# A hybrid decoder step with 64 routed experts: a sixth weight buffer in the place of the residual, and evictions ahead of the wait for weights

## The reference

```python
def sublayer_pair(x, c, mixer, w_ada, b_ada, g1, g2, g3, g4, moe_w):
    ...
    x = x + gt_m * rms_norm(m, g2)
    f = moe(rms_norm(x, g3) * (1 + sc_f) + sh_f, *moe_w)
    x = x + gt_f * rms_norm(f, g4)
    return x, new_state

def moe(h, w_router, router_bias, we_gate, we_up, we_down, ws_gate, ws_up, ws_down):
    ...
    _, top_idx = lax.top_k(scores + router_bias.astype(jnp.float32), TOP_K)
    top_w = top_s / jnp.sum(top_s, axis=-1, keepdims=True) * ROUTED_SCALE
    y = routed_experts(xf, top_idx, top_w, we_gate, we_up, we_down) + swiglu(xf, ws_gate, ws_up, ws_down)
```

## Time and profile before

| | |
|---|---|
| median of 3 runs | 1822.84 us (1821.18 to 1824.63) |
| profiled execution | 1818.75 us, its span 1817.0 us |
| TensorE (PE) busy | 1579.9 us, 87% |
| VectorE (DVE), ScalarE (ACT), GpSimd (POOL) busy | 29%, 23%, 17% |
| weights of 64 experts | 3 loads of 1024 KB each, 9.6, 11.8 and 8.7 us from issue to landing (median) |
| half copy of gate and up (L1982) | 52 times, 2294 ns |

### The profile page before, as it was taken

The page is one execution under the profiler, slowest core; times in us unless marked ns, Lnnn a source line. Parts: engine busy times, 40 slices in busy tenths (PEclk is TensorE's granted clock), DMA queues, the critical chain, the costliest instruction groups (busy, mean ns, idle before and its releaser), DMA issues.

```text
span 1817.0 us, 22427 instructions
## 1 busy us (share of the span) xinstructions
PE 1579.9 (87%) x7179; PEld 890.1 (49%) x7180; DVE 530.0 (29%) x951; ACT 410.7 (23%) x802; POOL 304.1 (17%) x322
## 2 busy tenths in 40 slices
PE   4389999999898999996888799899999998688955
PEld 1057888777755777773454233333333333222311
DVE  2120000146651111111664232323233232112227
ACT  2110000246430000002332132222232322112311
POOL 0030150002000000000111132222232221011244
PEclk8589999958989999998899899999999999888977
DMA  8882498164379743497152698988689988878487
GB/s 278 314 296 35 103 330 295 49 194 163 123 252 291 232 157 106 158 334 236 42 219 72 252 386 335 367 345 333 255 321 403 388 322 329 342 297 349 188 310 249
DMA packets 139202, 456.55 MB, mean 251 GB/s; under 512 B 13241, under 2 KB 78265, under 8 KB 109996
## 3 DMA queue, kind: packets, MB, share of 16 engines
q1 hardware_dynamic: 116541, 326.64, 49.1%
q0 software_dynamic: 22608, 129.18, 20.4%
HBM read 422.44 MB, written 106.92 MB: 291 GB/s over the span
## 4 chain that ended last, share of the span: by engine, by line
PE 76%; DMA 9%; issue 4%; SPq 3%; DVE 3%; POOL 2%; ACT 1%; another core or an unknown queue 1%; DVEq 0%; ACTq 0%; POOLq 0%
PE bank L2067 69%; DMA arena<-in_we_down 4%; PE bank L2596 3%; POOL arena L1148 2%; PE bank L2617 1%; SPq L780 1%; PE bank L2273 1%; DMA arena<-in_cache_b 1%; PE bank L2232 1%; DMA arena<-in_w_ada 1%; DMA arena<-in_w_in 1%; DMA mods<-arena 1%; DMA pscale<-in_pool_scale 1%; DMA yrows<-arena 1%
## 5 line engine op out<-in xcount | busy, mean ns | idle before, releaser
L2067 PE MATMUL bank<-arena 128*64 (+10 forms) x6096 | 1427.6, 517 | 144.8 <-DMA arena<-in_w_ada 30.2
L2067 PEld LDWEIGHTS bank<-arena 128*64 128x64 f32 (+3 forms) x6096 | 756.5, 174 | 714.4 <-issue 503.9
L1982 DVE COPY arena<-arena 128x4096 f32 x52 | 119.3, 2294 | 493.8 <-PE bank L2067 365.5
L1166 ACT ACTIVATE arena<-bank 128x512 f32<-128x512 f32 (+6 forms) x152 | 75.2, 505 | 355.2 <-PE bank L2067 219.7
L1106 POOL COPY icol<-arena 128x1 uint32 (+1 forms) x54 | 86.8, 1608 | 398.2 <-PE bank L2596 397.5
L1498 DVE COPY arena<-bank 128x512 f32<-128x512 f32 (+6 forms) x70 | 41.9, 606 | 210.5 <-PE bank L2067 186.1
L1420 ACT ACTIVATE arena<-arena 128x2048 f32 x52 | 99.3, 1910 | 13.3 <-issue 13.3
L1430 ACT ACTIVATE arena<-bank 128x256 f32<-128x256 f32 x52 | 20.0, 384 | 322.9 <-PE bank L2067 232.1
L1067 POOL DMA_DIRECT2D out<-in_cache_b x24 | 12.0, 507 | 447.2 <-PE bank L2067 446.9
L2596 PEld LDWEIGHTS bank<-ident,arena 128*128 128x128 f32 x416 | 51.0, 194 | 44.7 <-issue 44.7
L1305 ACT ACTIVATE arena<-bank 128x288 f32<-128x288 f32 x48 | 19.7, 411 | 233.6 <-PE bank L2067 233.6
(11 more groups left out here) (234 smaller groups left out, 709.2 us busy)
## 6 DMA issues: line engine op xcount, KB each, us to landing
arena<-in_we_gate SPq DMA_DIRECT2D x64, 1024.0 KB, 9.6
arena<-in_we_up SPq DMA_DIRECT2D x64, 1024.0 KB, 11.8
arena<-in_we_down SPq DMA_DIRECT2D x64, 1024.0 KB, 8.7
out<-in_cache_b POOLq DMA_DIRECT2D x8, 4080.0 KB, 15.0
yrows<-arena POOLq DMA_DIRECT2D x52, 512.0 KB, 9.2
arena<-in_w_ada SPq DMA_DIRECT2D x12, 2048.0 KB, 17.4
arena<-in_cache_b SPq DMA_DIRECT2D x18, 1024.0 KB, 7.9
arena<-in_w_in SPq DMA_DIRECT2D x7, 2048.0 KB, 15.4
```

Source lines behind the costliest of these rows:

```text
L1166: act.activation(out, pick(bank), ACT.Copy).then_inc(emptied["A"], 1)
L1982: dve.tensor_copy(whalf[:, 0:4096], arena[:, bass.ds(base, 4096)]).then_inc(gu_copied, 1)
L2067: return pe.matmul(out, lhsT, rhs, start=first, stop=last)
```

## The change

Three edits come together. The ring has six buffers; the sixth lies where `x1` was, so each tile of `x1` is also written to DRAM (`x1rows`) in the residual stage and loaded back when the sixth buffer's last expert is done. `ysh` moves into the fifth buffer and is loaded when that buffer's last expert is done, with the gates. In the loop, ScalarE loads the register values ahead of silu and waits for the weights behind its eviction; VectorE loads the address first and makes the half copy behind its eviction and the silu product. The tables for six buffers no longer fit one bank, so they take two (`bexp` 0 and 1).

```diff
-RING = 5
+RING = 6
...
-    fill(("bexp",), "D")
+    fill(("bexp", 0), "D")
+    fill(("bexp", 1), "D")
...
+        x1rows = nc.dram_tensor("x1rows", [TOK, D], F32, kind="Internal").ap()
...
-        ysh = mixed
+        ysh = at(A_W0 + 6144, TILES, D)
...
-        RING_AT = (A_W0, A_W1, A_M, 0, A_W0 + 6144)
+        RING_AT = (A_W0, A_W1, A_M, 0, A_W0 + 6144, A_ST + 6144)
...
-        g2mod = at(A_M + 2048, 2, D)
+        g2mod = [at(A_W0 + 6144 + TILES * D, D), at(A_ST + 6144, D)]
...
                 sp.dma_start(h2rows[toks(t), :], hbuf2[0:n, t % 2, :]).then_inc(h2_out, 16)
+                sp.dma_start(x1rows[toks(t), :], x1[0:n, t, :]).then_inc(x1_out, 16)
...
             expert_weights(4, slice(4, 5), None)
+            sp.wait_ge(x1_out, 16 * TILES)
+            sp.wait_ge(ysh_out[1], 32)
+            expert_weights(5, slice(5, 6), None)
...
+            for n in (4, 5):
+                e = NE - NE % RING - RING + n
+                done = sp.value_load(blocki[0:1, DONE + e:DONE + e + 1], min_val=2, max_val=NBLK + 2)
+                sp.wait_ge(d_done, done)
+                sp.sem_inc(load_ticks, 1)
+                if n == 4:
+                    for t in range(TILES):
+                        sp.dma_start(ysh[0:parts(t), t, :], yshared[toks(t), :]).then_inc(ysh_in, 16)
+                    sp.dma_start(g2mod[0], mods[0:1, 5, :].broadcast_to([P, D])).then_inc(g2_in, 16)
+                else:
+                    for t in range(TILES):
+                        sp.dma_start(x1[0:parts(t), t, :], x1rows[toks(t), :]).then_inc(x1_in, 16)
+                    sp.dma_start(g2mod[1][0:NS, :], sample_rows(5)).then_inc(g2_in, 16)
...
             sp.sem_inc(weights_idle, 1)
-            for t in range(TILES):
-                sp.dma_start(ysh[0:parts(t), t, :], yshared[toks(t), :]).then_inc(ysh_in, 16)
-            sp.dma_start(g2mod[:, 0, :], mods[0:1, 5, :].broadcast_to([P, D])).then_inc(g2_in, 16)
-            sp.dma_start(g2mod[0:NS, 1, :], sample_rows(5)).then_inc(g2_in, 16)
...
-            def weights_wait(i, off):
-
-                due = [act.value_load(entry(i, off + DUE + NBLK * n), min_val=1, max_val=NE // RING + 2)
-                       for n in range(RING)]
+            def weights_due(i, off):
+
+                return [act.value_load(entry(i, off + DUE + NBLK * n), min_val=1, max_val=NE // RING + 2)
+                        for n in range(RING)]
+
+            def weights_wait(due):
+
                 for n in range(RING):
                     act.wait_ge(wexp_in[n], 48 * due[n])
                 act.sem_inc(weights_in, 1)
...
             with act.Fori(0, last) as i:
                 for off in (1, 2):
                     turned(i, off - 1)
-                    weights_wait(i, off + 1)
+                    due = weights_due(i, off + 1)
                     silu(i, off)
                     rows(i, off + 1)
+                    weights_wait(due)
                     result(i, off - 1)
...
-            empty(("bexp",), blocki[0:1, 0:DONE], lambda b: b[0:1, 0:DONE])
-            wait_emptied(dve, ("bexp",))
+            for n in range(2):
+                empty(("bexp", n), blocki[0:1, DONE // 2 * n:DONE // 2 * (n + 1)], lambda b: b[0:1, 0:DONE // 2])
+            wait_emptied(dve, ("bexp", 1))
...
-            def copy_gate_up(i, off):
+            def lower_base(i, off):
+
+                return dve.value_load(entry(i, off + NBLK), min_val=0, max_val=RING_AT[2])
+
+            def copy_gate_up(base, i, off):
 
                 dve.wait_ge(weights_in, 2 * i + off + 1)
-                base = dve.value_load(entry(i, off + NBLK), min_val=0, max_val=RING_AT[2])
                 dve.tensor_copy(whalf[:, 0:4096], arena[:, bass.ds(base, 4096)]).then_inc(gu_copied, 1)
...
             with dve.Fori(0, last) as i:
                 for off in (1, 2):
-                    dve.wait_ge(gu_done, 2 * i + off + 2)
-                    copy_gate_up(i, off + 1)
+                    base = lower_base(i, off + 1)
                     rows_half(i, off + 1)
                     product(i, off)
+                    copy_gate_up(base, i, off + 1)
                     result(i, off - 1)
...
                         dve.wait_ge(g2_in, 16 * 2)
+                        dve.wait_ge(x1_in, 16 * TILES)
```

More of the change, by code:

```diff
@@ L510, in build @@
         tabi = arena[:, A_R + 2952:A_R + 2953].bitcast(I32)
[L511 to L514, removed]
+        sixes = at(A_R + 2780, 16)
+        ringrow = at(A_R + 2796, RING)
+        sidehot = at(A_R + 2804, 2, RING)
+        donei = arena[0:1, A_R + 2820:A_R + 2820 + NE].bitcast(I32)
         weigh = at(A_R + 2964, TOPK * NE)
@@ L585, in build @@
                              "at_ready", "d_done", "y_act", "y_dve"))
+        x1_out, x1_in = sem("x1_out"), sem("x1_in")
         weights_in, g2_in, g_used = sem("weights_in"), sem("g2_in"), sem("g_used")
@@ L665, in build @@
         blocki = arena[:, A_R + 2144:A_R + 2144 + DONE + NE].bitcast(I32)
-        assert DONE <= 512 and 2144 + DONE + NE <= 2720
+        assert DONE <= 1024 and 2144 + DONE + NE <= 2780
         def wait_keys_used(eng, f):
@@ L1445, in _ @@
             act.wait_ge(ysh_out[1], 32)
-            weights_wait(0, 0)
+            weights_wait(weights_due(0, 0))
             rows(0, 0)
-            weights_wait(0, 1)
+            due = weights_due(0, 1)
             silu(0, 0)
             rows(0, 1)
+            weights_wait(due)
             with act.Fori(0, last) as i:
@@ L1894, in _ @@
                 dve.memset(ringrow[:, n:n + 1], float(RING_AT[n]))
-            link(dve.tensor_scalar(fives, iota[:, 0:16], float(RING), None, ALU.mult))
+            link(dve.tensor_scalar(sixes, iota[:, 0:16], float(RING), None, ALU.mult))
             link(dve.tensor_scalar(iotab, iota[:, 0:NBLK], float(P), None, ALU.mult))
@@ L1940, in _ @@
             for n in range(2):
-                link(dve.tensor_scalar(prod[:, NE * n:NE * n + 13], fives[:, 0:13], order[:, n:n + 1], None,
+                link(dve.tensor_scalar(prod[:, NE * n:NE * n + 13], sixes[:, 0:13], order[:, n:n + 1], None,
                                        ALU.is_le, ALU.add, accum_out=quo[:, n:n + 1]))
@@ L1953, in _ @@
             link(dve.tensor_scalar(blocki[0:1, DONE:DONE + NE], donei, 7, None, ALU.logical_shift_right))
-            link(dve.tensor_scalar(bexpf[:, 7:8], ends[:, NE - 1:NE], 255.0, None, ALU.add))
+            link(dve.tensor_scalar(bexpf[:, 8:9], ends[:, NE - 1:NE], 255.0, None, ALU.add))
             one_hots(3)
-            link(dve.tensor_copy(tabi, bexpf[:, 7:8]))
+            link(dve.tensor_copy(tabi, bexpf[:, 8:9]))
             link(dve.tensor_scalar(pairs[:, 0:1], tabi, 8, None, ALU.logical_shift_right))
@@ L2004, in _ @@
             dve.sem_inc(y_dve, 1)
-            copy_gate_up(0, 0)
+            copy_gate_up(lower_base(0, 0), 0, 0)
             rows_half(0, 0)
-            dve.wait_ge(gu_done, 2)
-            copy_gate_up(0, 1)
+            base = lower_base(0, 1)
             rows_half(0, 1)
             product(0, 0)
+            copy_gate_up(base, 0, 1)
             with dve.Fori(0, last) as i:
                 for off in (1, 2):
-                    dve.wait_ge(gu_done, 2 * i + off + 2)
-                    copy_gate_up(i, off + 1)
+                    base = lower_base(i, off + 1)
                     rows_half(i, off + 1)
                     product(i, off)
+                    copy_gate_up(base, i, off + 1)
                     result(i, off - 1)
@@ L2056, in _ @@
                         dve.wait_ge(g2_in, 16 * 2)
-                    link(dve.scalar_tensor_tensor(y, y, st, g2mod[0:r, s, :], ALU.mult, ALU.mult))
+                        dve.wait_ge(x1_in, 16 * TILES)
+                    link(dve.scalar_tensor_tensor(y, y, st, g2mod[s][0:r, :], ALU.mult, ALU.mult))
                     dve.tensor_tensor(x1[0:r, u, :], x1[0:r, u, :], y, ALU.add).then_inc(f_out, 1)
@@ L2571, in _ @@
             block_rows(4)
-            bank = bank_for(pe, ("bexp",))
             pe.wait_ge(bexp_ready, 1)
             for n in range(2 + RING):
-                ins = mm(bank[0:1, n * NBLK:(n + 1) * NBLK], bexpf[:, n:n + 1], ident[:, 0:NBLK], True, True)
-            close(ins)
+                m = n % 4
+                if m == 0:
+                    bank = bank_for(pe, ("bexp", n // 4))
+                ins = mm(bank[0:1, m * NBLK:(m + 1) * NBLK], bexpf[:, n:n + 1], ident[:, 0:NBLK], True, True)
+                if m == 3:
+                    close(ins)
             shared_down(3)
```

## The result

| | before | after |
|---|---|---|
| median of the runs | 1823.74 us (1821.18 to 1825.07, 4 runs) | 1746.03 us (1743.38 to 1752.75, 4 runs) |
| profiled execution, span | 1818.75 us, 1817.0 us | 1746.22 us, 1744.5 us |
| TensorE busy | 1579.9 us, 87% | 1574.5 us, 90% |

The ratio is 0.9585, 95% interval 0.956 to 0.961.

The account below looks back on a forecast made before the run. TensorE's own pace was taken as the bound, 12.63 us per block, with halts where the weight ring is full. From 1818.75: -56.2 + 6 - 6.3 = -56.5 gives 1762.2; the median stands 4.1 above: 1766, range 1753 to 1792.

Parts of the forecast that it names:

- the cost per block where nothing halts: Expert loop, new order: half copy stays covered by the down product, so 0 per block; a gain was excluded.
- halts (-56.2, residue +6): Expert loop waits for `we_down`: 56.2 us of excess go with the sixth buffer and new order, 6 us remain: -50.
- tail: Loop's end: with the loads gone ahead, the last yrows store lands in 2.9 us, not 9.2: -6.3 us.
- start: Ahead of block 0: one register load, +0.45, against VectorE's, -0.52, and two-table fill: 0; x1 stores hidden.
- My upper bound: Blocks 37 to 48: transfers need 164 us against 151.6 of blocks, so without lead 12.4 us of halts would stay.
- the six halts: Chain of before: `we_down` landings of 12 to 13 us at 1163.69, 1606.02 and four more between them.
- Copy and gather: Rival: VectorE's half copy and GpSimd's gather collide on the shared port, 0.35 us in about 45 blocks: 1782; chance 0.08.
- Rivals: Slot buys little, 1788, 0.12; copy and gather collide, 1782, 0.08; slot buys nothing, 1799, 0.04; half copy on path, 1830, 0.04.
- the three signs of being wrong: Blocks without a halt above 12.8 us; the half copy in each block's chain; halts left at more than three blocks.

Follow-up runs that it names:

- e1: The kernel before, five buffers, with only the changed order on ScalarE and VectorE (half copy last, behind eviction and product): 1789.61 us, ratio 0.9792.
- e3: The kernel before, with TensorE's register load of the next gate/up weights' place moved ahead of the silu-product wait in every second block: 1818.35 us, ratio 0.9966.
- e4: The changed kernel, with VectorE's half copy between the eviction and the silu product instead of behind the product: 1783.1 us, ratio 0.976.
- e7: The kernel before, with TensorE's register load ahead of each gate/up product made twice: 1857.52 us, one run.
- e8: The changed kernel, with TensorE's register load ahead of each gate/up product made twice: 1746.21 us, one run.
- e2: The changed kernel (six buffers, x1 stores, early loads) with ScalarE's and VectorE's order as before: 1765.81 us, ratio 0.9687.
- e5: The changed kernel, with the loads of yshared, x1 and gate rows put back behind the expert loop's end: 1758.98 us, ratio 0.9628.
- e6: The changed kernel, with down-weight loads from the seventh expert on fetching 0.5 MB instead of 1 MB, so the output is wrong: 1738.74 us, ratio 0.953.

## Why the prediction was wrong

The step that failed is the cost per block where nothing halts: "I take 0 per block; a gain is excluded, since TensorE has no wait there to lose." It had one. In the terms of the sum:

| | predicted, us | measured, us | from |
|---|---|---|---|
| halts (-56.2, residue +6) | -50.2 | -46.2 | excess 59.7 to 13.5 |
| undisturbed blocks | 0 | -23.1 | 50 x (12.59 - 12.13) |
| tail | -6.3 | -5.7 | store to end of span, 83.2 to 77.5 |
| last down product and its store | 0 | -1.7 | 6.81 to 5.11 us from one to the other |
| start | 0 | +4.3 | block 1 at 1023.93 and 1028.19 |
| sum | -50.2 - 6.3 = -56.5 | -72.4 | spans 1817.0 and 1744.5: -72.5 |

- **Blocks.** The earlier trace rows ended with "0.21 <-issue" and I read it as TensorE's own pace. Three things stood against that. "Issue" is time for which the profile shows no cause, not work. The two kinds of block, 12.41 and 12.77, differed on the same matmuls, so something other than matmuls set them. And the product ended 0.52 us before the two turns started, with a register load and four waits in the program behind their wait. I saw the product as free because the turns were not late, and did not ask what stands behind the turns' wait in TensorE's order, though I did so for ScalarE and VectorE. The runs of e1, e3, e4 and the pair e7 and e8 show the mechanism from both sides.
- **Halts.** Right in mechanism, nearly in size. The buffer alone took 49.1 us (e2: 59.7 to 10.6), against -50.2. With the shorter block the excess is 13.5 (11.4 and 11.6 in e5 and e8) and not the 6 I took. My upper bound shows why: 164 us of transfers stood against 12 blocks, 151.6 us at 12.63 but 145.6 at 12.13. The profiles have the same trend: 6.6 at 12.85, 10.6 at 12.59, 11.4 to 13.5 at 12.13. That is also the likely reason why the two halves, 33.1 and 49.1 us in the loop, give 69.3 together: what the order saves at the halts has little left to act on, and the faster block runs sooner into the DMA engines. In my reading of the chain of before, the six halts have only three between 1163.69 and 1606.02 and one behind (1641.13), and the landing at 1576.46 takes 6.55 us, not 12 to 13; the excess that I took from the blocks does not depend on it.
- **Copy and gather.** The copy won. On the page of after, the gather's instruction takes 2733 ns on average and the index copy 178, against 1059 and 1608 before. The gather is late with a block to spare, which was the harmless branch of that rival. In the timeline above the instruction ends at 1321.15, 0.91 us after the copy (1320.24), close to its old 1.04. That is as the Trainium skill ("SBUF — State Buffer", section "Who interferes with whom") has it: one of the two blocks the other.
- **Tail.** 6.3 was right for the landing: 2.88 against 9.20 us, and 8.96 again in e5. From that store to the end of the span it is 83.2 to 88.7 us in the four kernels with late loads and the old ring (before, e1, e3, e7), and 77.2 to 83.5 in the five with early loads, so the 5.7 in the sum is one pair out of such a spread.
- **Last down product.** The 1.7 us are the clock: behind the same 2.86 us of idle the product takes 5.35 us at a granted clock of 0.68 before, and 3.65 at 1.00 after. Every other profile has 5.3 us or more, also those with the sixth buffer and the new order (e5, e8), so this part is luck of one execution.
- **Start.** Not settled. Block 0 starts at 1009.16, 1013.23, 1005.56 and 1021.39 in the four programs with five buffers (before, e1, e3, e7) and between 1009.15 and 1017.65 in six with six buffers (after, e2, e4, e5, e6, e8). The second range lies inside the first, so the 4.3 us can't be told from differences between executions. A shift of a few us by the x1 stores or the second table could hide in that; it was not tried by itself.
- **Rivals.** None of the four came about; all lay on the wrong side, and so did the three signs of being wrong, none of which appeared (halts are left at three blocks: 1541.74, 1594.56, 1622.12). The range had no room below, because the sum allowed no term for a faster block.

No kernel tried here that does all the work is faster than the changed one. From block 2 to 1539 us its loop is TensorE without a pause, and behind that, up to 1625 us, DMA bandwidth.

## What to carry to other kernels

"Issue" between two matmuls is a question: look at what stands behind the last semaphore wait in that engine's program order (register loads, further waits), and when that wait was over. A producer that ends just as its consumer can start is not free of cost; it has to end earlier by as much as the consumer's engine has to do in order behind that wait, here 1.2 to 1.6 us before the next product can start. When blocks that do the same work alternate in length, the difference may be such overhead; here it was, and went whole.

## What the runs showed of the hardware that was not expected

- A register load on TensorE from the on-chip table costs 0.62 to 0.69 us when it stands bare behind a wait (e7), against 0.53 for each of ScalarE's five in a row and 0.63 for VectorE's one in the chain of before ahead of block 0, and nothing when it stands under running matmuls (e8).
- The block across the loop's end takes another 0.36 us on the same path (12.77 against 12.41 us), and that too vanishes under cover: in after both kinds of block take 12.13. What at the loop's end takes it, no run shows by itself.
- A load takes 25.61 us to land when the queue ahead of it is full, and the chain names that one load; with the DMA engines at 1.01 over the stretch the time belongs to all transfers in it.
